# Retention's input projection: four units begun together, and the first weight block split at the end of the expert layer

## The reference

```python
f = moe_ffn(tok, router_w, router_b, moe_w1[layer], moe_w3[layer], moe_w2[layer])
hc = hc + g2c * f[:n_c].reshape(hc.shape)        # the residual of the expert layer
h = h + g2 * f[n_c:].reshape(h.shape)
...
xm = modulate(rmsnorm(h, norm_g[layer, 0]), sh1, sc1)    # layer 1
cm = modulate(rmsnorm(hc, norm_g[layer, 0]), sh1c, sc1c)
ql, kl, vl, gl = split(xm @ w_in)                # w_in: 1024 x 6144
qc, kc, vc, gc = split(cm @ w_in)
```

## Time and profile before

| | us |
|---|---|
| median of 3 runs | 1808.79 |
| lowest and highest run | 1807.18, 1810.28 |
| profiled execution: span from the first to the last instruction | 1808.2 |
| PE busy | 1700.5 (94%) |
| DVE busy | 1148.0 (63%) |
| ACT busy | 996.0 (55%) |
| POOL busy | 66.2 (4%) |
| mean granted clock of PE, share of full | 0.976 |

### The profile page before, as it was taken

One profiled execution on the slowest core, in us unless ns is written; L12 is line 12 of the kernel. 1 busy time (PEld: TensorE's weight loads), 2 busy tenths in 40 slices (PEclk: granted clock), 3 DMA queues, 4 the chain that ended last, 5 costly groups with the idle time before them and its releaser, 6 DMA issues.

```text
span 1808.2 us, 30073 instructions
## 1 busy us (share of the span) xinstructions
PE 1700.5 (94%) x12284; PEld 1452.8 (80%) x12284; DVE 1148.0 (63%) x1529; ACT 996.0 (55%) x1314; POOL 66.2 (4%) x66
## 2 busy tenths in 40 slices
PE   6999989899999959999998799999989999999898
PEld 4787666788888838888988588888868998897688
DVE  5341664799898756333345599898965577544564
ACT  4322653588888735124343388888844573354452
POOL 0000000000000010000000000000010000100100
PEclk9999999999999979999999899999989999999999
DMA  8645005799999882223573389999964445264512
GB/s 331 205 124 233 1 7 225 300 408 405 406 406 405 354 316 94 94 93 140 187 273 147 139 355 405 410 407 406 392 253 149 179 148 188 67 226 151 150 61 70
DMA packets 52845, 420.84 MB, mean 233 GB/s; under 512 B 17012, under 2 KB 18164, under 8 KB 30336
## 3 DMA queue, kind: packets, MB, share of 16 engines
q1 hardware_dynamic: 26416, 364.55, 51.1%
q0 software_dynamic: 8304, 31.64, 5.5%
q10 hardware_dynamic: 18016, 23.07, 3.7%
HBM read 398.22 MB, written 21.02 MB: 232 GB/s over the span
## 4 chain that ended last, share of the span: by engine, by line
PE 83%; DVE 7%; DMA 4%; ACT 3%; issue 2%; POOL 0%; SPq 0%; DVEq 0%; ACTq 0%; POOLq 0%
PE ps L742 47%; PE ps L893 18%; PE ps L703 4%; DMA ring<-w_all 3%; PE ps L726 2%; PE ps L902 1%; PE ps L749 1%; PE ps L909 1%; PE ps L1134 1%; PE ps L1406 1%; PE ps L1163 1%; PE ps L1138 1%; DMA arena<-y_d,tok_row 1%; PE ps L1149 1%; PE ps L794 1%
## 5 line engine op out<-in xcount | busy, mean ns | idle before, releaser
L2257 DVE TENSOR_TENSOR w_lo<-ring,w_hi 128x1024 fp32r<-128x1024 f32 x384 | 452.3, 1219 | 51.2 <-ACT w_hi L1629 49.9
L1629 ACT ACTIVATE w_hi<-ring 128x1024 fp32r<-128x1024 f32 x384 | 395.0, 1056 | 101.7 <-PE ps L893 53.1
L742 PE MATMUL ps<-XT_lo,arena_r 128*128 128x256 f32 (+1 forms) x1712 | 386.6, 301 | 5.3 <-DVE ring_r L2128 3.9
L742 PEld LDWEIGHTS ps<-XT_lo,arena_r 128*128 128x128 f32 x1712 | 281.8, 190 | 21.2 <-issue 7.9
L893 PE MATMUL ps<-w_hi,x_hi 128*128 128x256 f32 (+1 forms) x768 | 249.1, 324 | 4.2 <-issue 3.7
L893 PE MATMUL ps<-w_hi,x_lo 128*128 128x256 f32 (+1 forms) x768 | 245.1, 319 | 0.0
L893 PE MATMUL ps<-w_lo,x_hi 128*128 128x256 f32 (+1 forms) x768 | 245.0, 319 | 0.0
L742 PE MATMUL ps<-arena_r 128*128 128x512 f32 (+1 forms) x656 | 234.0, 365 | 9.6 <-DVE arena_r L2413 3.5
L2128 DVE TENSOR_TENSOR ring_r<-ring,arena_r 128x1024 fp32r<-128x1024 f32 x96 | 113.7, 1222 | 111.5 <-ACT arena_r L1531 111.2
L742 PE MATMUL ps<-XT_lo,ring_r 128*128 128x256 f32 x640 | 179.5, 280 | 0.0
L893 PEld LDWEIGHTS ps<-w_hi,x_hi 128*128 128x128 f32 x768 | 146.2, 190 | 22.0 <-issue 6.2
(11 more groups left out here) (351 smaller groups left out, 2665.5 us busy)
## 6 DMA issues: line engine op xcount, KB each, us to landing
ring<-w_all SPq DMA_DIRECT2D x172, 2048.0 KB, 9.9
y_d<-arena ACTq DMA_DIRECT2D x32, 512.0 KB, 10.1
arena<-toep_d POOLq DMA_DIRECT2D x16, 384.0 KB, 12.0
arena<-rpb ACTq DMA_DIRECT2D x16, 192.0 KB, 3.9
xtok_d<-arena ACTq DMA_DIRECT2D x6, 512.0 KB, 3.3
hT<-h SPq DMA_DIRECT2D x2, 1024.0 KB, 6.3
arena<-cb_d POOLq DMA_DIRECT2D x1, 1536.0 KB, 13.2
arena<-cc_d POOLq DMA_DIRECT2D x1, 959.0 KB, 7.1
```

Of the source, the lines that this page charges most:

```text
L742: last = nc.tensor.matmul(out, a, b, start=(first and i == 0), stop=(final and i == 2))
L1629: nc.scalar.activation(w_hi[:, q], slot(b, "p (q c) -> p q c", q=4)[:, q], ACT.Copy).then_inc(hi_rdy, 1)
L2257: nc.vector.tensor_tensor(w_lo[:, q], slot(base + n, "p (q c) -> p q c", q=4)[:, q], as_f32(w_hi[:, q]), ALU.subtract).then_inc(*split_sig ...
```

## The change

- ACT splits the weights p = 0 to 3 at the end of the routed expert layer of layer 0, behind `rows_out(14, 3)` and ahead of `table(ACT.Sqrt)` and the squares; DVE writes their lo behind the last residual row, ahead of `late_mods`. The dense path gets the same.
- Their hi goes to columns 18432 to 22527 of the arena, a place of its own; POOL's fetch of `cb`, which lands there, now waits for unit 3 (`rp_mm` 4). The hi of p = 4 to 7 needs no wait.
- PE begins with units 0 to 3 together: for each x row it does three matmuls for each of the four units.
- Behind the x rows ACT and DVE split p = 4 to 7 (DVE 4 and 5 ahead of the reciprocal of the context half, 6 and 7 behind its multiplies). ACT reads units 0 to 3 without work between, and makes the context's x hi two rows at a time in units 4 to 7, both copies each.

```diff
         def ret_hi(p):
-            buf = ret_w[p % 4 if p < 32 else 4 + (p - 32) % 3]
+            buf = area_r(18432 + 1024 * p, 1024) if p < 4 else ret_w[p % 4 if p < 32 else 4 + (p - 32) % 3]
...
         def ret_free(p):
-            if p < 4 or p == 32:
+            if p < 8 or p == 32:
                 return None
...
                 if layer == 0:
+                    pool.wait_ge(rp_mm, 4)
                     pool.dma_start(cb, cb_d).then_inc(ld_cb, 16)
...
-            unit = 0
-            for b in range(12):
+            for k in range(KT):
+                pe.wait_ge(nm_lo, LO_RET + k + 1)
+                for m in range(4):
+                    if k == 0:
+                        pe.wait_ge(dw_lo, DW_RET + m + 1)
+                    last = three_terms(ps[:, m, 0:SEQ], ret_hi(m)[:, k], part_of(B_RET, m, False, ring_r)[:, k],
+                                       ret_x[1][:, k], XT_lo[:, k, LAT], k == 0, k == KT - 1)
+                    if k == KT - 1:
+                        last.then_inc(rp_mm, 1)
+            release(B_RET)
+            unit = 4
+            for b in range(1, 12):
...
@@ ACT, routed(layer)
                 else:
                     for p in range(4):
                         z_split(p)
+                if layer == 0:
+                    for p in range(4):
+                        ret_split(p)
                 table(ACT.Sqrt)
                 for m in range(KT):
...
@@ ACT, retention
-            ret_split(0)
             for k in range(KT):
                 norm_hi(2, k, 1, k, ret_x[1], both=k % 2)
-                if k == 1:
-                    ret_split(1)
-            for p in range(2, 4):
+            for p in range(4, 8):
                 ret_split(p)
...
             for u in range(48):
-                if u < KT:
-                    norm_hi(2, u, 0, KT + u, ret_x[0])
+                if 4 <= u < KT:
+                    for k in (2 * u - 8, 2 * u - 7):
+                        norm_hi(2, k, 0, KT + k, ret_x[0], both=True)
                 act.wait_ge(rp_mm, u + 1)
...
-                if u + 4 < 48:
+                if 4 <= u < 44:
                     ret_split(u + 4)
...
@@ DVE, retention
-                if k == 1:
-                    ret_split(0)
-            ret_split(1)
+            for p in range(4, 6):
+                ret_split(p)
             link(nc.vector.reciprocal(inv_rms[:, CTX], inv_rms[:, CTX]))
             for k in range(KT):
                 nc.vector.tensor_tensor(XT[:, k, CTX], hT[:, k, CTX], inv_rms[:, CTX], ALU.mult).then_inc(nm_tmp, 1)
-            ret_split(2)
-            ret_split(3)
+            for p in range(6, 8):
+                ret_split(p)
...
-            for u in range(KT):
-                norm_lo(2, u, 0, KT + u, ret_x[0])
-                ret_split(u + 4)
+            for u in range(4):
+                for k in (2 * u, 2 * u + 1):
+                    norm_lo(2, k, 0, KT + k, ret_x[0], scaled=True)
+                ret_split(u + 8)
```

More of the change, by code:

```diff
@@ L1215, in _ @@
                         for k in range(KT):
-                            if unit in (0, 8):
+                            if unit == 8:
                                 pe.wait_ge(nm_lo, LO_RET + unit + k + 1)
@@ L1596, in router, with ret_split @@
                     rows_out(12, 0)
+            def ret_split(p):
+                n = B_RET + p // 4
+                if p % 4 == 0:
+                    act.wait_ge(w_full[n % SLOTS], 16 * (n // SLOTS + 1))
+                if ret_free(p):
+                    act.wait_ge(*ret_free(p))
+                nc.scalar.activation(ret_hi(p), part_of(n, p % 4, p // 4 in RET_V, ring), ACT.Copy).then_inc(dw_hi, 1)
             def late_mods():
@@ L2140, in norm_partial, with ret_split @@
                     last.then_inc(nm_part, 1)
+            def ret_split(p):
+                n = B_RET + p // 4
+                dve.wait_ge(dw_hi, DW_RET + p + 1)
+                nc.vector.tensor_tensor(part_of(n, p % 4, p // 4 in RET_V, ring_r), part_of(n, p % 4, p // 4 in RET_V, ring),
+                                        as_f32(ret_hi(p)), ALU.subtract).then_inc(dw_lo, 1)
             def late_mods():
@@ L2519, in norm_lo @@
                 nc.vector.tensor_tensor(XT_lo[:, k, seg * SEQ:(seg + 1) * SEQ], part, as_f32(hi[:, k]), ALU.subtract).then_inc(nm_lo, 1)
[L2521 to L2526, removed]
             norm(2)
```

## The result

The changed kernel takes **1821.28 us** (median of 4 runs, 1820.77 to 1822.12) against 1808.20 for the kernel before (4 runs, 1807.18 to 1810.28): 13.1 us more, a ratio of 1.0077 with a 95% interval of 1.0063 to 1.0092. Repeated on another chip the ratio was 1.0092 (1.0069 to 1.0115). It is slower, as forecast (1823.8, range 1817.0 to 1831.0).

The account below looks back on a forecast made before the run. PE was taken to bound the kernel, at 83% of the chain that ended last. 16.0 - 3.4 + 2.4 = +15.0 us on the 1808.2 span gave 1823.2; with the median 0.6 above the span, 1823.8 us, range 1817.0 to 1831.0.

Parts of the forecast that it names:

- The three terms: Root 16.0 us later, root to unit 4 shorter by 3.4, low clock in units 4 to 7 costing 2.4.
- The wait for block 71: ACT's early splits wait until 664.6 for their weights, holding table load, squares and root behind them: root 16.0 us later.
- the lower of the two rows I took: Clock recovery in the sums: rows showed 4.1 and about 5.5 us of work; 4.8 was taken, 2.4 lost.
- The table load: Behind ACT's four splits: load and dummy activation, hidden before, now on the path at 1.49 us, without further drain.
- DVE's early lo splits at nothing: Four lo splits behind the residual, 4.7 us, cost nothing ahead of the root; up to 1 if cover is short.
- Unit 4 at root + 21.9: ACT's reading of unit 0, behind Ln and DVE's decays' step, releases unit 4 then, instead of 25.3: gain 3.4 us.
- The clock at unit 4: PE idles 5.7 us ahead of unit 4, so its clock falls: 2.4 us lost in units 4 to 7.
- DVE sets the pace: From the last x row at T + 11.35, DVE rather than PE determines when unit 4 can start, T + 21.9.
- The intended gain: Rival: block 71 landed before the first square, splits fall into ACT's idle time: -1.0 us, or -3.4 without clock loss; 8%.
- The norm chain that never regains its clock: Rival: the sums of squares stay at low clock throughout and take 21.6 us: +8.4 more, 1832.2 us; 9%.
- the joint start that keeps PE slow: Rival: changing banks every three matmuls in units 0 to 3 loses PE its clock: +20.8, 1829.6 us; 8%.

Follow-up runs that it names:

- e1: Changed kernel with block 71 fetched ahead of the held block 70 in SP's order: 1805.23 us, ratio 0.9983 to the kernel before.
- e2: Kernel before with only the edit of e1 to SP's order of loads: 1808.63 us, ratio 1.0006 to the kernel before.
- e4: Changed kernel with units 0 to 3 one after another instead of row by row: 1819.99 us, ratio 1.0062 to the kernel before.
- e5: The changed kernel itself run again, nothing edited: 1823.19 us, ratio 1.0092 to the kernel before.
- e6: Changed kernel with the hold on block 70 moved from the third to the fourth combined tile: 1822.80 us, ratio 1.0086 to the kernel before.
- e9: e1 with units 0 to 3 one after another: 1804.75 us, ratio 0.9984 to the kernel before.
- e11: Changed kernel with 56 dummy matmuls on PE behind the transposes of row 3: 1815.96 us, ratio 1.0045 to the kernel before.
- e7: Changed kernel with the decays' Exp and Ln behind unit 7's split, DVE's step behind its context rows: 1817.59 us, ratio 1.0057 to the kernel before.
- e8: Changed kernel with the edits of both e1 and e7: 1801.13 us, ratio 0.9964 to the kernel before.
- e10: e8 with units 0 to 3 one after another: 1803.93 us, ratio 0.9978 to the kernel before.
- e12: e8 with 26 dummy matmuls instead of 16 ahead of the first x row: 1798.47 us, ratio 0.9954 to the kernel before.

## Why the prediction was right

The three terms were 16.0, -3.4 and +2.4, and measured 15.3, -3.7 and +1.6. Each came out a little lower, none hides another, so the sum isn't right by luck.

**The wait for block 71.** Right, and shown: e1 takes it away with one edit to the order of loads and takes the whole excess away (ratio 1.0077 to 0.9983, some 17 us; 14.9 of them stand in the trace as the root's place behind ACT's last copy, 53.48 to 38.63), and e2 shows that the edit alone does nothing. Landing was forecast 34.9 us behind ACT's last copy, 34.4 measured; splits 3.90 and 3.89; the first square done at 40.9 and at 40.4. The sums behind it were forecast at 13.2 and took 682.13 - 669.08 = 13.05, with the clock low up to 673.2, 4.1 us of them, as in the lower of the two rows I took. Together 15.3, where I had 16.0: the landing and the table load were taken 0.5 too long, the sums with their clock 0.15.

**The table load.** It cost 1.28, and the activation began 0.02 us behind its end. The drain of some 1.4 us more, of the Trainium skill's page "ScalarE: Activation LUTs" (section "What ACT_TABLE_LOAD costs"), doesn't show here as it didn't before.

**DVE's early lo splits at nothing.** Right: 4.62 us, over at 682.02, and the reciprocal began as usual 0.9 behind the root.

**Unit 4 at root + 21.9.** 21.63 measured, and 21.62 to 21.64 in every kernel that splits early and keeps the decays' place (e1, e4, e5, e6, e9, e11). The new wait for ACT's reading is shown by e7, which takes it away and gains 5.6 us. One working on record is wrong, though its value is right: a quarter of one weight copy (1.99 for two) is 0.25, not 0.5. A context copy did take 0.5 before (688.47 to 688.97 in ACT's order), and with it the terms add up to 21.8.

**The clock at unit 4.** The mechanism was right, the size off: 1.6 instead of 2.4. PE idled 4.29, not 5.7, because it began the first row 1.0 us later than forecast (below) and so ended later; the clock came back after some 3.5 us of work, not 4.8.

**What the sum hid.** The edit that names the change, the joint start, had no term of its own in my sum, only "DVE sets the pace". e4 and e9 bear that out: unit 4 came earlier because four lo splits had left DVE's chain and ACT's reading no longer had work between, not because PE took the rows jointly. I hadn't said that the joint form would cost something, the clock's 1.5 us.

**The rivals.** The intended gain was there once the block was (e1: -2.7 us by the medians, where I gave -1.0 to -3.4). The norm chain that never regains its clock and the joint start that keeps PE slow didn't occur. All 96 matmuls of the joint start ran at full clock in the changed kernel. In e8 it was low for 3.4 us, but came back with the joint start still running, and it fell in forms with one unit after another as well (the kernel before, e9, e10). So changing banks didn't keep PE slow in any run here.

## What to carry to other kernels

Work moved into an engine's idle time must have its data by then: look in the loading queue for the block it reads, and for a hold on any block ahead of it, since the in-order engine then holds everything behind that one instruction. Fetching one block ahead of another was worth 15 us here, and moving nothing else turned a loss of 0.8% into a gain of 0.2%. And when the engine that was waited for gets faster, ask who is read next: an early end of unit 3 was worth nothing until ACT's reading of it no longer stood behind a wait for a third engine.

## What was unexpected

- **PE starts its first row late.** The dummies are the last work inside the conditional block of the routed path, and the retention stands behind it. The first x row's lo was ready at 686.87 (root + 4.7), but PE's first matmul began at 687.81, and at root + 6.55 in e5, where the profile says "issue" after 3.00 us idle. In the kernel before, the first row waited for a weight's lo as well, so this didn't show. In e11 it was at root + 7.12. It costs nothing in the changed kernel, but in e7 and e8, where unit 4 follows PE's own end, some 1.2 us (an estimate: the first matmul was at root + 5.9, not 4.7). In e12 the dummies ended at 671.94, behind the row's arrival at root + 4.7 (671.0), and PE still idled 1.96 us. What makes it wasn't tried.
- **The same gap, different clocks.** Behind 2.38 us idle ahead of unit 0 the clock stayed up in e7 and fell for 3.4 us in e8. It stayed up behind 2.13 in the changed kernel and behind 3.00 in e5, and fell behind 2.19 in e10 and 2.40 in the kernel before. In the joint form the price was 0 to 1.6 us; with one unit after another it stayed low for 3.3 us (e9), 6.8 us (e10) or 10.3 us (before). So the length of the gap doesn't settle it, and what does wasn't found.
- **The early load didn't disturb the gathers.** In e1 block 71's 2 MB went out at 629.62, 2.9 us ahead of POOL's first indirect DMA, and landed at 637.5 among them, and the third tile was combined within 0.7 us of its place before, in all six kernels with that order.
